# Twelve modulation chunks of a two-block transformer kernel, summed on VectorE during the MLPs instead of multiplied on TensorE during attention

## The reference, cut to what matters

```
mod = (silu(c) @ ada_w[l] + ada_b[l])              # 1024 x 6144, six vectors of 1024
shift_m, scale_m, gate_m, shift_f, scale_f, gate_f = split(mod, 6)
h = rms_norm(x) * (1 + scale_m) + shift_m
...                                                # two attentions, two branches, gates
x = x + gate_m * y
h = rms_norm(x) * (1 + scale_f) + shift_f
x = x + gate_f * (relu(h @ w_mlp_up[l])**2 @ w_mlp_down[l])
...
# second block: silu(c_lat) @ mod_w + mod_b and silu(c_ctx) @ mod_w + mod_b
```

## Time and profile before

| | |
|---|---|
| median of 3 executions | 2990.07 us (2983.64, 2990.07, 2999.83) |
| the profiled execution | 2982.92 us, of which the span in the trace is 2981.1 us |
| TensorE busy | 2635.8 us, 88% of the span |
| VectorE busy | 837.4 us, 28% |
| ScalarE busy | 544.3 us, 18% |
| GpSimd busy | 107.6 us, 4% |
| granted TensorE clock, mean | 0.913 of full |

### The profile page before, as it was taken

The page is one execution under the profiler, slowest core; times in us unless marked ns, Lnnn a source line. Parts: engine busy times, 40 slices in busy tenths (PEclk is TensorE's granted clock), DMA queues, the critical chain, the costliest instruction groups (busy, mean ns, idle before and its releaser), DMA issues.

```text
span 2981.1 us, 37067 instructions
## 1 busy us (share of the span) xinstructions
PE 2635.8 (88%) x15664; PEld 1862.3 (62%) x15664; DVE 837.4 (28%) x1487; ACT 544.3 (18%) x1080; POOL 107.6 (4%) x116
## 2 busy tenths in 40 slices
PE   6999999999999899999979899999877877777776
PEld 4757577887757578887658788785433333333333
DVE  2633421101634421102466453213111111111112
ACT  2115411001116311101223432102000000000001
POOL 0100000000100000000011110000000000000000
PEclk8999999999999999999988888898878778887889
DMA  7335745445332546343000001336999999999998
GB/s 301 113 137 231 281 170 198 155 156 198 113 133 93 180 168 231 128 164 115 29 1 2 1 1 58 120 145 251 427 428 428 429 429 428 427 429 429 429 428 364
DMA packets 48593, 666.72 MB, mean 224 GB/s; under 512 B 5498, under 2 KB 5669, under 8 KB 7520
## 3 DMA queue, kind: packets, MB, share of 16 engines
q1 hardware_dynamic: 46528, 656.65, 54.7%
q0 software_dynamic: 1952, 8.40, 0.8%
HBM read 663.98 MB, written 1.05 MB: 223 GB/s over the span
## 4 chain that ended last, share of the span: by engine, by line
PE 68%; DMA 24%; DVE 4%; ACT 2%; issue 1%; POOL 0%; DVEq 0%; POOLq 0%
PE bank L2528 57%; DMA ring<-exp_w 22%; PE bank L2536 7%; PE bank L2540 2%; PE bank L1765 1%; DMA arena<-exp_w 1%; DMA arena<-x 1%; PE bank L2557 1%; PE bank L1791 1%; ACT hT L2091 0%; DVE ring L1348 0%; DVE arena L1248 0%; DVE arena L2251 0%; DVE stat L2444 0%; ACT arena L2096 0%
## 5 line engine op out<-in xcount | busy, mean ns | idle before, releaser
L2528 PE MATMUL bank<-hT,ring 128*128 128x256 f32 (+2 forms) x3232 | 742.7, 391 | 9.6 <-ACT hT L2091 6.3
L2528 PEld LDWEIGHTS bank<-hT,ring 128*128 128x128 f32 x3232 | 614.4, 195 | 140.7 <-issue 60.8
L2536 PE MATMUL bank<-ring,arena 128*32 128x512 f32 (+1 forms) x2528 | 303.5, 616 | 139.9 <-DMA ring<-exp_w 138.0
L2528 PE MATMUL bank<-arena,ring 128*128 128x256 f32 (+1 forms) x1920 | 419.0, 380 | 5.9 <-POOL arena L2063 2.8
L2528 PEld LDWEIGHTS bank<-arena,ring 128*128 128x128 f32 (+1 forms) x1920 | 363.2, 190 | 59.4 <-POOL arena L2063 3.6
L2536 PEld LDWEIGHTS bank<-ring,arena 128*32 128x32 f32 x2528 | 82.6, 119 | 304.8 <-issue 193.3
L2528 PE MATMUL bank<-arena 64*128 64x128 f32 (+5 forms) x1252 | 243.7, 377 | 18.9 <-DVE arena L1341 11.3
L2536 PE MATMUL bank<-arena 128*32 128x256 f32 (+1 forms) x1552 | 176.1, 612 | 74.2 <-DMA arena<-exp_w 60.1
L2528 PEld LDWEIGHTS bank<-vec,arena 128*128 128x128 f32 x1344 | 183.4, 219 | 81.9 <-issue 74.7
L2528 PEld LDWEIGHTS bank<-arena 64*128 64x128 f32 (+2 forms) x1252 | 162.6, 193 | 90.5 <-issue 71.8
L2528 PE MATMUL bank<-vec,arena 128*128 128x32 f32 (+2 forms) x1344 | 189.6, 294 | 4.7 <-ACT arena L2096 4.7
(11 more groups left out here) (304 smaller groups left out, 1862.8 us busy)
## 6 DMA issues: line engine op xcount, KB each, us to landing
ring<-exp_w SPq DMA_DIRECT2D x126, 2048.0 KB, 26.5
arena<-exp_w SPq DMA_DIRECT2D x65, 2048.0 KB, 25.6
ring<-w_in SPq DMA_DIRECT2D x38, 2048.0 KB, 8.2
ring<-ada_w SPq DMA_DIRECT2D x24, 2048.0 KB, 10.0
ring<-w_mlp_up SPq DMA_DIRECT2D x16, 2048.0 KB, 8.2
ring<-w_mlp_down SPq DMA_DIRECT2D x16, 2048.0 KB, 8.1
ring<-mod_w SPq DMA_DIRECT2D x12, 2048.0 KB, 8.2
ring<-w_out SPq DMA_DIRECT2D x6, 2048.0 KB, 8.1
```

The lines of the kernel that those rows point to most:

```text
L2528: mm = nc.tensor.matmul(out_, a, b, start=(i == 0), stop=(i == len(pairs) - 1))
L2536: mm = nc.tensor.matmul(o, a, b, start=(i < 4), stop=(i >= len(pairs) - 4))
```

## The change

Of the next modulation, seven chunks of layer 0 (2 to 8) and five of layer 1 (4 to 8) leave the attention phase. The chunks of layer 0 go to the even steps 0 to 12 of `up`, those of layer 1 to steps 0 to 4 of `down`. Their raw product on TensorE and its copy on ScalarE go. In their place VectorE multiplies the chunk with the vector as a scalar per partition and sums the eight tiles into one row of 128x512 (one tensor_scalar, seven scalar_tensor_tensor, each waiting for the one before). TensorE adds up the partitions with the four instructions of the pick, their moving operand now one column of ones, and waits for `mod_summed` first. Chunks 0 and 1 of layer 0 stand in turn 10 now, chunk 3 of layer 1 in turn 10. The order of weight loads follows. For the five chunks of `mod` only the latent vector's column is computed; three small products of `norm2_pre`, `norm1_post` and `norm2_post` on VectorE move behind the long convolution.

```diff
-    own = {0: {8: [0], 9: [1], 10: [2, 3], 12: [4, 5], 14: [6], 16: [7], 18: [8], MLP_NORM: [9, 10, 11]},
-           1: {MIX_NORM: [0, 1, 2], 9: [3], 10: [4], 12: [5], 14: [6], 16: [7], 18: [8], MLP_NORM: [9, 10, 11]}}
+    own = {0: {10: [0, 1], MLP_NORM: [9, 10, 11]},
+           1: {MIX_NORM: [0, 1, 2], 10: [3], MLP_NORM: [9, 10, 11]}}
...
+def mlp_modulations(l, what, i):
+
+    at = {0: {("up", 2 * n): 2 + n for n in range(7)},
+          1: {("down", n): 4 + n for n in range(5)}}[l]
+    return [(*next_modulation(l), at[what, i])] if (what, i) in at else []
...
-        cols("up", "w_mlp_up", l, 0, D_FF)
-        cols("down", "w_mlp_down", l, 0, D, rows=D_FF, step=128)
+        for n in range(8):
+            modulation_chunks(mlp_modulations(l, "up", 2 * n))
+            out.append((("up", l, n), "w_mlp_up", l, 0, D, 512 * n, 512))
+        for n in range(8):
+            modulation_chunks(mlp_modulations(l, "down", n))
+            out.append((("down", l, n), "w_mlp_down", l, 0, D_FF, 128 * n, 128))
...
+            def mlp_sums(l, what, i):
+
+                for key in mlp_modulations(l, what, i):
+                    n = chunk_at[key]
+                    if l == 0:
+                        dve.wait_ge(cond_ready, 4)
+                    dve.wait_ge(slot_loaded[slot_of(n)], 16 * loads(n))
+                    w, row = slot_view(key), sum_row(l, key[2])
+                    of = (lambda k: cond(0)[:, k, 0:1]) if l == 0 else (lambda k: amp[:, 5, k:k + 1])
+                    chain(v.tensor_scalar(row, w[:, 0], of(0), None, ALU.mult))
+                    for k in range(1, KT):
+                        ins = v.scalar_tensor_tensor(out=row, in0=w[:, k], scalar=of(k), in1=row, op0=ALU.mult, op1=ALU.add)
+                        if k < KT - 1:
+                            chain(ins)
+                    ins.then_inc(mod_summed, 1)
...
                 for i in range(16):
+                    mlp_sums(l, "up", i)
                     b = filled(dve, ("up", l, i))
 
                     dve.wait_ge(relu_ready, 16 * l + i + 1)
                     r = ar(A_QK + 512 * i, 512)
                     free(v.tensor_tensor(r, r, b[:, :], ALU.mult), ("up", l, i))
+                    mlp_biases(l, "up", i)
...
+            def mlp_columns(l, what, i):
+
+                for key in mlp_modulations(l, what, i):
+                    summed[0] += 1
+                    b = start(key)
+                    pe.wait_ge(mod_summed, summed[0])
+                    for j in range(4):
+                        mm = product(b[:, j:j + 1], [(sum_row(l, key[2])[:, j * P:(j + 1) * P], col("ones"))])
+                    finish(mm)
...
                     columns(("up", l, i), w, (2 * (i % 2), 2 * (i % 2) + 1), h_of if i == 0 else lambda k: hT[:, 0, k], KT)
+                    mlp_columns(l, "up", i)
```

More of the change, by code:

```diff
@@ L199, in cols, with modulation_chunks @@
             out.append(((name, l, n), array, l, 0, rows, c, min(step, c1 - c)))
+    def modulation_chunks(now):
+        for name, nl, c in now:
+            out.append(((name, nl, c), "ada_w" if name == "ada" else "mod_w_2", nl, 0, D, 512 * c, 512))
     def side(l, turn):
-        for name, nl, c in side_modulations(l, turn):
-            out.append(((name, nl, c), "ada_w" if name == "ada" else "mod_w_2", nl, 0, D, 512 * c, 512))
+        modulation_chunks(side_modulations(l, turn))
     for c in ADA_ORDER:
@@ L455, in __init__ @@
                 add(("up", l, i), "v", [("up", l, i // 2)] if i % 2 else [])
+                for key in mlp_modulations(l, "up", i):
+                    add(key, "v", [key])
                 for step in context_steps(l, i):
@@ L459, in __init__ @@
                 add(("down", l, j), "v", [("down", l, j)])
+                for key in mlp_modulations(l, "down", j):
+                    add(key, "v", [key])
     def add(self, key, engine, chunks=()):
@@ L713, in mod_row, with sum_row, mod_target @@
             return ar(A_WORK + 5120 + 512 * (jobs.row[key] % 4), 512)
+        def sum_row(l, c):
+            return ar((A_WORK + 5120 if l == 0 else B_HF) + 512 * (c % 2), 512)
+        def mod_target(name, nl, c, n):
+            to, bias = (mods[nl % 2], ("ada_b", nl)) if name == "ada" else (mod, "mod_b")
+            return to[:, 4 * c:4 * c + 4, 0:n], wide(cols_of(bias)[:, 4 * c:4 * c + 4], n)
         def cond(i):
@@ L751, in build @@
         relu_ready = sem("relu_ready")
+        mod_summed = sem("mod_summed")
         gated, mix_ready = sem("gated"), sem("mix_ready")
@@ L1227, in second_vector @@
             v.tensor_tensor(z, z, u[:, 4:8], ALU.mult).then_inc(z_ready, 1)
+            emptied(dve, ("mod", 0, 8))
+            chain(v.scalar_tensor_tensor(out=amp[:, 2, :], in0=mod[:, 32:40, 0], scalar=1.0, in1=cols_of("norm2_pre"),
+                                         op0=ALU.add, op1=ALU.mult))
+            for i, g, s in ((3, "norm1_post", 16), (4, "norm2_post", 40)):
+                chain(v.tensor_tensor(amp[:, i, :], mod[:, s:s + 8, 0], cols_of(g), ALU.mult))
             keep = stat[:, 16:30]
@@ L2115, in _ @@
                 nc.scalar.activation(to, wide(cols_of(name), to.shape[2]), ACT.Silu).then_inc(cond_ready, 1)
+            nc.scalar.activation(amp[:, 5, :], cols_of("c_lat"), ACT.Silu).then_inc(cond_ready, 1)
             act.wait_ge(angles_ready, 1)
@@ L2266, in modulations, with mlp_biases @@
                     key = (name, l, c)
-                    to, bias = (mods[l % 2], ("ada_b", l)) if name == "ada" else (mod, "mod_b")
                     n = 1 if name == "ada" else 2
+                    to, bias = mod_target(name, l, c, n)
                     b = filled(dve, key)
-                    free(v.tensor_tensor(to[:, 4 * c:4 * c + 4, 0:n], b[:, 0:4 * n].rearrange("p (a b) -> p a b", b=n),
-                                         wide(cols_of(bias)[:, 4 * c:4 * c + 4], n), ALU.add), key)
+                    free(v.tensor_tensor(to, b[:, 0:4 * n].rearrange("p (a b) -> p a b", b=n), bias, ALU.add), key)
                 before[:] = now
+            def mlp_sums(l, what, i):
[12 more added lines that the diff above has]
+                    ins.then_inc(mod_summed, 1)
+            def mlp_biases(l, what, i):
+                for key in mlp_modulations(l, what, i):
+                    to, bias = mod_target(*key, 1)
+                    b = filled(dve, key)
+                    free(v.tensor_tensor(to, b[:, 0:4].rearrange("p (a b) -> p a b", b=1), bias, ALU.add), key)
             def context(what, n):
@@ L2281, in context @@
                     emptied(dve, ("mod", 0, 11))
-                    for i, g, s, w in ((0, "norm1_pre", 8, 0), (1, "norm1_pre", 8, 1), (2, "norm2_pre", 32, 0)):
-                        chain(v.scalar_tensor_tensor(out=amp[:, i, :], in0=mod[:, s:s + 8, w], scalar=1.0, in1=cols_of(g),
+                    for i, w in ((0, 0), (1, 1)):
+                        chain(v.scalar_tensor_tensor(out=amp[:, i, :], in0=mod[:, 8:16, w], scalar=1.0, in1=cols_of("norm1_pre"),
                                                      op0=ALU.add, op1=ALU.mult))
-                    for i, g, s in ((3, "norm1_post", 16), (4, "norm2_post", 40)):
-                        chain(v.tensor_tensor(amp[:, i, :], mod[:, s:s + 8, 0], cols_of(g), ALU.mult))
                     norm("ctx", 0, ar(B_CT, KT, SEQ), lambda k: amp[:, 1, k:k + 1], hT[:, 1])
@@ L2494, in _ @@
                 for j in range(8):
+                    mlp_sums(l, "down", j)
                     b = filled(dve, ("down", l, j))
@@ L2497, in _ @@
                                                 op0=ALU.mult, op1=ALU.add), ("down", l, j))
+                    mlp_biases(l, "down", j)
             second_vector(dve, chain, free, norm)
@@ L2576, in modulations @@
                 before[:] = now
+            summed = [0]
+            def mlp_columns(l, what, i):
+                for key in mlp_modulations(l, what, i):
+                    summed[0] += 1
[4 more added lines that the diff above has]
+                    finish(mm)
             def context(what, n):
@@ L2772, in _ @@
                     columns(("down", l, j), w, (0,), lambda k: ar(A_QK, 32, SEQ)[:, k], 32)
+                    mlp_columns(l, "down", j)
             second_tensor(pe, start, finish, chunk, product, four_sums, turn, columns, norm, normed, done)
```

## The result

Twenty executions of each kernel: before 2983.56 us median (2976.02 to 3002.04), after 2995.01 us (2993.14 to 3006.63). The ratio is 1.0031, 95% interval 1.0019 to 1.0043: 0.2 to 0.4% slower. The profiled execution took 2994.92 us, 12.0 more than that of before.

A forecast was written before the change was run, and what follows sets the result against it. TensorE's path up to the experts was taken as the bound. Terms 10.8 + 3.9 + 0.3 + 0.1 - 15.7 = -0.6 us, plus 14.1 us of clock falls, gave +13.5 us on 2989.1: 3003 us, own range 2992 to 3012, wider 2984 to 3019.

The forecast's parts named there:

- Out of attention, 15.7 us: Both attention phases: removed raw products and picks gain 10.5 us in layer 0 and 5.2 us in layer 1.
- `on` to `on` in layer 0: Turns 8 and 9: two raw products and one pick fewer, gaining 3.65 us of 14.01 us.
- The floor from scores to transposes: Attention steps 2, 4, 6: VectorE's mask, maximum and normalise set 3.95 us, whatever TensorE does meanwhile.
- A raw product at 1.86 us: TensorE: cost of one chunk's raw product at full clock, read from the next job starting at 380.11 at the earliest.
- Picks in the MLP: Between MLP steps: each of twelve chunks still costs TensorE four pick instructions, 0.9 us each, 10.8 us in all, uncovered.
- The stall: `up` of layer 0: TensorE waits 0.65 us for VectorE's 6.0 us sum at six steps, 3.9 us.
- The rival that had it grow over the edge: `up`: a sum 0.6 us longer brings up to six more clock falls, +14 us, 3016 us; chance 0.17.
- The ring: Load slots shared by `up` and modulation chunks: first `up` load lands late, 0.3 us once; `down` loads close but hidden.
- The clock: Steps 2, 4, 6 of both layers: emptied gaps make TensorE's granted clock fall six times, 2.35 us each, 14.1 us.
- The rule on idle gaps: Skill's warning covers only gaps longer than any new one; by it no clock fall comes and the sum stays -0.6 us.
- No change is within 0.5%, 15 us, about what a measurement of this kernel can tell: Whole kernel: bound for calling the outcome the same; chances faster 0.06, same 0.57, slower 0.37.
- the forecast's own 0.55: Whole kernel: chance of the main case, six clock falls or nearly; 0.19 of it to more than 15 us slower.

The follow-up runs named there:

- e9: Changed kernel with one real raw product kept in each of the six gaps, the other six chunks summed on VectorE, four in layer 0's `down`; 2969.13 us, ratio 0.9960.
- e7: Changed kernel with VectorE's sums for even steps of `up` issued before the odd step's square instead of behind it; 2992.25 us, ratio 1.0004.
- e5: Changed kernel with two useless 128x512 products on TensorE in steps 2, 4 and 6 of each layer; 2981.45 us, ratio 0.9974.
- e4: Changed kernel with layer 0's seven sums moved from even steps of `up` to steps 0 to 6 of `down`; 2992.13 us, ratio 1.0015.
- e2: Changed kernel cut to one half: only the seven chunks of steps 2, 4 and 6 leave attention; 3000.05 us, ratio 1.0040 to before.
- e6: Changed kernel with one useless 128x512 product on TensorE in steps 2, 4 and 6 of each layer; 2984.47 us, ratio 0.9976.
- e8: Changed kernel with layer 0's sums in `down` (e4) and two useless products in each gap (e5); 2976.04 us, ratio 0.9958.
- e10: The kernel of e8 once more, timed beside e9 on one chip; 2973.27 us, ratio 0.9975 to before.
- e1: Changed kernel with four useless 128x512 products on TensorE in steps 2, 4 and 6 of each layer; 2986.53 us, ratio 0.9993.
- e3: Changed kernel cut to the other half: only five chunks, of turns 8, 9 and 18, move; raw products of steps 2, 4, 6 stay; 2982.64 us, ratio 0.9981.

## Why the prediction was right or wrong

The mechanism and the sum, +13.5 us for 11.5 measured between the medians, were right; the outcome that I named as the likeliest, no change, was not. The steps of the sum were measured one by one.
- *Out of attention, 15.7 us.* `on` to `on` in layer 0 is now 333.66 - 323.32 = 10.34 us, a gain of 3.67 for 3.65 predicted. The floor from scores to transposes held at 3.95 us in all six steps; e9 shows the other side of it: in five of its six gaps the raw product stands there for nothing. From `on` to `branchB`, without the falls, layer 1 gained 5.1 us (+1.5 less 6.6) for 5.2 predicted, and layer 0 12.3 us (-4.7 less 7.6), of which 1.5 is a better clock in turn 10 that nobody predicted; 10.8 is left for 10.5.
- *A raw product at 1.86 us.* The time holds (in rows 5 the transposes start at 415.54, and the raw product ahead of them started at 413.68), but not the reading given for it: by rows 4 the product ends at 378.25 + 1.92 = 380.17, not at 380.11.
- *Picks in the MLP.* A step of `down` with a pick takes 14.70 us (1294.72 to 1309.43) for 13.82 without, so a pick costs 0.88 us, for 0.9: 10.6 us in all for 10.8.
- *The stall.* The wait is 0.57 us at six places, for 0.65 predicted, but each costs 0.82 us by the timelines of after and e7: 4.9 us for the 3.9 of the sum. The rival that had it grow over the edge is out: the MLP had no fall behind a stall of 0.57 us and a pick.
- *The ring.* The expected 0.3 us didn't show as a wait for a load in after; in e5, where `up` begins 7 us sooner, its first product waits 0.41 us for `w_mlp_up`. Loads in `down`, called close, were in time in e4 as well.
- *The clock.* Six falls of six, 14.2 us by e5, for 14.1. That the 2.35 us apiece, taken as the middle of two rows, hit the mean is in part luck. Single falls cost 1.1 us (18.71 - 17.62) to 2.8 us, and the same gaps, which lost the clock in all 18 cases of e2, e4 and e7 as well, cost 13.9, 15.7 and 15.8 us there, reckoned in the same way from `branchA` to `branchA`.
- *The rule on idle gaps* of the Trainium skill (TensorE: Matmul & The Clock Gate, the section on oscillation), by which no fall comes in gaps as short as these, would have given -0.6 us. The measurement decides against it: the clock fell in gaps of 2.40 us between light work six times of six in after, and in gaps of 1.34 us twice in six in e6.

What was wrong is the step from the sum to the chances. **"No change is within 0.5%, 15 us, about what a measurement of this kernel can tell"** led me to call no change the likeliest outcome, 0.57, for a sum of +0.45%. With that bound I gave only 0.19 of the forecast's own 0.55 to slower. Twenty executions of each tell 0.2% from nothing: the interval of the change is 0.19 to 0.43%, all of it slower, though within the 0.5%. For the forecast that I had, slower was the outcome to name. Connected with it, the base was the mean of four executions, 2989.1 us. Twenty have their median at 2983.6, and the profiled one's own 2982.9 was the better guess; on it the sum gives 2996.4, where 2995.0 was measured, while the 3003 on record is 8 us too high.

What the sum did not have is the clock away from the six gaps: +1.7 us in `wo`, +1.5 in the first step of `up`, +2.3 in the first step of `down` in layer 1 (16.20 us to its pick, for 13.90 in the steps behind it), against -1.5 in turn 10 (its two raw products take 4.11 us for 5.64), -0.6 from the norm of layer 1 to `down`, and -4.9 near 1890 us. They come to -1.5 us together. That single terms of up to 4.9 us nearly cancel, and that the sum came so close to the measurement with them left out, is luck. Whether they belong to the change or to where in time its work happened to lie isn't settled.

## What to carry to other kernels

Work that fills a wait of TensorE, and ends before the wait does, is free twice: it cost no time here, and in 39 of 42 cases the clock stayed up. Before taking it out, look at what stands behind it in the timeline; if that is a wait of another engine, the time goes there, and the granted clock of the next stretch may fall. Take out the work that stands on the path (here turns 8, 9 and 18, and half of step 2) and leave the rest. Idle time in the profile can be less than what a stall costs (0.57 us for 0.82 here), so measure from start to start. A change of half a per cent is told apart if there are executions enough; say what the sum says.

## What was not expected of the hardware

- A single 128x512 float32 product, 0.88 us, in a gap of 2.46 us kept the clock in four of six cases in the one profiled execution of e6. Two products (1.76 us) kept it in 17 of 18 cases (e5, e8, e10).
- The clock also fell with no gap at all. In step 2 of layer 0 of e1, e9 and e10 TensorE was busy all through with picks of one column, transposes and 64-row scores, and the products behind them ran at a clock of 0.70, 0.54 and 0.54. The kernel before, e3, e5 and e8 came through the same place at full clock.
- One of these products costs 0.88 us at full clock, two records of 0.43 and more; I had reckoned with half.
- In layer 0 the kernels after, e3, e4, e5, e6 and e7 lost the clock at the start of `wo` too, behind 14 us of products of only 64 rows and a wait of 1.4 us; the kernel before, e1, e2, e8, e9 and e10 did not, with the same products and the same wait. So a single profile doesn't tell whether such a place falls.
